# Windowed attention of the hybrid layers: from single steps of full-array products to pairs of steps of 64-row and 64-column tiles

## The reference

```python
# 8 query heads of 64, 2 key/value heads, blocks of 128 tokens
scores = jnp.einsum('bnqhgd,bnkhd->bnhgqk', qb, kcat).astype(jnp.float32)   # own block and the one before
scores = jnp.where(valid[None, :, None, None], scores * (HEAD_DIM ** -0.5), MASK_VALUE)
probs = jax.nn.softmax(jnp.concatenate([scores, sink], axis=-1), axis=-1)[..., :-1]
out = jnp.einsum('bnhgqk,bnkhd->bnqhgd', probs.astype(v.dtype), vcat)
...
gates = jax.nn.sigmoid(gate_logits)         # one of the projections of x, in three branches
merged = gates0 * (o_a @ w_a) + gates1 * (o_b @ w_b) + gates2 * (o_c @ w_c)
x = layer_norm(ALPHA * x + merged @ w_o)    # then the gated, convolved MLP
```

## Time and profile before

| | us |
|---|---|
| median of 3 runs | 2805.62 (2803.07 to 2809.05) |
| the profiled execution, its own time | 2806.11 |
| its span in the trace | 2804.3 |
| PE busy | 2785.4 |
| ACT busy | 1760.6 |
| DVE busy | 1698.9 |

### The profile page before, as it was taken

How to read it: one execution, slowest core, us unless ns; L and a number is a source line. 1 busy time by engine, 2 the same in 40 slices (tenths; PEclk the granted TensorE clock), 3 DMA queues, 4 the chain that set the end, 5 groups by cost and what they waited for, 6 DMA issues and landing times.

```text
span 2804.3 us, 42771 instructions
## 1 busy us (share of the span) xinstructions
PE 2785.4 (99%) x15770; PEld 2436.0 (87%) x15770; DVE 1698.9 (61%) x3003; ACT 1760.6 (63%) x2565; POOL 408.3 (15%) x472
## 2 busy tenths in 40 slices
PE   9999999999999999999999999999999999999999
PEld 7989889889998688899988898799988889789997
DVE  6654637354553773644547675678848766657864
ACT  7666767566655774565656755666656765566664
POOL 1111111111111001111111111111111011111110
PEclk9999999999999999999999999999999999999999
DMA  9766768688888327888886688788887578798885
GB/s 249 165 151 146 170 134 176 143 198 188 191 185 199 78 59 178 183 192 189 191 191 147 143 191 192 176 179 191 197 194 173 119 171 186 174 199 182 193 195 114
DMA packets 137038, 481.66 MB, mean 172 GB/s; under 512 B 15344, under 2 KB 15600, under 8 KB 136720
## 3 DMA queue, kind: packets, MB, share of 16 engines
q0 software_dynamic: 67296, 227.77, 46.3%
q1 hardware_dynamic: 68688, 249.59, 30.2%
q10 hardware_dynamic: 864, 1.72, 0.2%
HBM read 476.92 MB, written 2.10 MB: 171 GB/s over the span
## 4 chain that ended last, share of the span: by engine, by line
PE 98%; ACT 1%; DVE 1%; issue 0%; DVEq 0%; ACTq 0%
PE ps L1513 49%; PE ps L1689 24%; PE ps L1532 5%; PE ps L1965 3%; PE ps L2036 3%; PE ps L2091 2%; PE ps L1632 1%; PE ps L1902 1%; PE ps L2138 1%; PE ps L2116 1%; PE ps L1487 1%; PE ps L1809 1%; PE ps L1593 1%; PE ps L1615 0%; PE ps L1891 0%; PE ps L1590 0%
## 5 line engine op out<-in xcount | busy, mean ns | idle before, releaser
L573 ACT ACTIVATE wh<-raw 128x1024 fp32r<-128x1024 f32 (+2 forms) x461 | 455.5, 988 | 570.2 <-PE ps L1513 431.6
L556 POOL DMA_DIRECT2D wl<-weights x465 | 406.4, 874 | 2361.2 <-ACT wl L578 2301.4
L578 ACT ACTIVATE wl<-raw 128x1024 fp32r<-128x1024 f32 (+2 forms) x461 | 450.8, 978 | 0.0
L1513 PE MATMUL ps<-HH,wh 128*128 128x512 f32 x1088 | 427.2, 393 | 1.5 <-issue 1.3
L1513 PE MATMUL ps<-HH,wl 128*128 128x512 f32 x1088 | 423.8, 390 | 0.0
L1513 PE MATMUL ps<-HL,wh 128*128 128x512 f32 x1088 | 423.6, 389 | 0.0
L1513 PE MATMUL ps<-MH,wh 128*128 128x512 f32 x928 | 362.4, 390 | 2.9 <-issue 2.2
L1513 PE MATMUL ps<-MH,wl 128*128 128x512 f32 x928 | 361.2, 389 | 0.0
L1513 PE MATMUL ps<-ML,wh 128*128 128x512 f32 x928 | 361.1, 389 | 0.0
L1513 PEld LDWEIGHTS ps<-HH,wh 128*128 128x128 f32 x1088 | 204.3, 188 | 45.9 <-issue 4.0
L1513 PEld LDWEIGHTS ps<-HH,wl 128*128 128x128 f32 x1088 | 204.2, 188 | 43.0
(11 more groups left out here) (452 smaller groups left out, 5673.7 us busy)
## 6 DMA issues: line engine op xcount, KB each, us to landing
raw<-weights SPq DMA_DIRECT2D x468, 512.0 KB, 5.1
wl<-weights POOLq DMA_DIRECT2D x329, 512.0 KB, 7.9
wl<-weights POOLq DMA_DIRECT2D x136, 384.0 KB, 6.6
XT<-x SPq DMA_DIRECT2D x4, 512.0 KB, 8.3
arena<-tables POOLq DMA_DIRECT2D x1, 1024.0 KB, 11.0
out<-XT SPq DMA_DIRECT2D x1, 768.0 KB, 3.3
out<-XT SPq DMA_DIRECT2D x3, 256.0 KB, 2.4
arena<-table_h ACTq DMA_DIRECT2D x1, 640.0 KB, 5.9
```

The costliest lines, as they stand in the source:

```text
L556: pool.dma_start(wl[:, n, first:], weights[slab][:, first:], accum_op=ALU.add).then_inc(w_lo[n], 16)
L573: act_f(wh[:, n, at:w], raw[:, n, at:w], ACT.Copy)
L578: act_f(wl[:, n, at:w], raw[:, n, at:w], ACT.Identity, scale=-1.0).then_inc(w_hi, 1)
L1513: op = mm(bank(g, t), w[:, slot, at:at + P], x[:, first + kt, :], start=(kt == 0 and w is wh and x is xh), stop=(kt == n_k - 1 and w is wl ...
```

## The change

The 16 steps become 8 pairs of steps (two token blocks of one query tile).

- Scores: the key tile is one tile kH with both heads' rows and no zeros. Each head's product contracts its own 64 rows, so the two heads' products stand in different halves of the array's rows. Head h writes PSUM bank 4 + h, step s of the pair at column 256 s.
- Outputs: each head's product writes 64 columns of the array (64 partitions of PSUM) and takes only that head's 64 value columns. The two steps of a pair lie beside each other in one bank.
- Semaphores, statistics and copies go by pairs: the statistics are 4 columns wide where they were 2, the copies out of PSUM, the rounding and the low part 256 columns where they were 128. The exponentials and the transposes stay by step.
- The probability buffers are four where they were three. The scores' two banks are the same for each pair, where before they alternated.
- On PE a pair issues: its scores, the outputs of the pair two before, a gate tile, the transpose of a step of the pair before, a gate tile, the other transpose. Four memsets on DVE (the zeros) are gone.

```diff
-    return 2 if i < 4 else 1 if i <= H_STEPS else 0
+    return (4, 0, 0) if pair == 0 else (3, 0, 0) if pair == 1 else (1, 1, 0) if pair < H_PAIRS else (1, 1, 1)
...
-            return ps[:, h_bank(g, 4 + j % 2), h * w:(h + 1) * w]
+            return ps[:, h_bank(g, 4 + h), 256 * s:256 * s + w]
...
+                    else:
+                        pe.wait_ge(att_m, (a + 2 * pair).value(0))
+                    for s, n in h_steps(pair):
+                        keys = slice(max(n - 1, 0) * P, (n + 1) * P)
+                        for h in range(2):
+                            rows = slice(64 * h, 64 * h + 64)
+                            op = mm(h_scores(gate, s, h, h_width(n)), qh[rows, t, n * P:(n + 1) * P], kH[rows, keys],
+                                    start=True, stop=True)
+                    op.then_inc(att_s, 2)
...
+                def outputs(pair):
+                    pe.wait_ge(att_c, (a + 2 * pair).value(2))
+                    if pair > 0:
+                        pe.wait_ge(att_out, hl.times(H_STEPS).value(2 * pair))
+                    for s, n in h_steps(pair):
+                        per = h_width(n) // P
+                        for k in range(per):
+                            for h in range(2):
+                                at, cols = (h * per + k) * P, slice(64 * h, 64 * h + 64)
+                                op = mm(h_out(gate)[cols, s * P:(s + 1) * P], vzH[:, h, n - per + 1 + k, cols],
+                                        pTH[:, s, at:at + P], start=(k == 0), stop=(k == per - 1))
+                    op.then_inc(att_o, 2)
...
-                for i in range(H_STEPS + 3):
-                    if i < H_STEPS:
-                        score(i)
-                    done = gate_tiles(done, gate_tiles_at(i))
-                    if 2 <= i < H_STEPS + 2:
-                        transpose(i - 2)
-                    if i >= 3:
-                        output(i - 3)
-                    if i == H_STEPS + 1:
-                        gate_tiles(done, 1)
+                for pair in range(H_PAIRS + 2):
+                    tiles_at = gate_tiles_at(pair) if pair <= H_PAIRS else (0, 0, 0)
+                    if pair < H_PAIRS:
+                        scores(pair)
+                    if pair >= 2:
+                        outputs(pair - 2)
+                    done = gate_tiles(done, tiles_at[0])
+                    if 1 <= pair <= H_PAIRS:
+                        transpose(2 * pair - 2)
+                    done = gate_tiles(done, tiles_at[1])
+                    if 1 <= pair <= H_PAIRS:
+                        transpose(2 * pair - 1)
+                    done = gate_tiles(done, tiles_at[2])
...
+                for pair in range(H_PAIRS + 2):
+                    if pair < H_PAIRS:
+                        most(pair)
+                    if pair <= H_PAIRS:
+                        stats(pair if pair < H_PAIRS else None, pair - 1 if pair else None)
+                    for work in beside.get(pair, ()):
+                        work()
+                    if pair >= 2:
+                        low_parts(pair - 2)
```

More of the change, by code:

```diff
@@ L96 @@
 H_STEPS = 16
+H_PAIRS = H_STEPS // 2
+H_STATS = ("most", "less", "sum", "sink", "gap")
 HALVES = (slice(0, 256), slice(256, 512))
@@ L439, in h_out @@
             base = h_bank(g, 7) * S
-            return psf[:, base:base + P]
+            return psf[:, base:base + 2 * P]
         def a_window(i):
@@ L2104, in mix, with scores @@
                             .then_inc(mix_done, 1)
[L2106 to L2110 removed]
+                def scores(pair):
+                    t = pair // 2
+                    if pair == 0:
                         pe.wait_ge(qh_done, hl.times(5).value(5))
                         pe.wait_ge(mix_taken, hl.times(2).value(2))
[L2113 to L2121 removed]
+                    else:
[7 more added lines that the diff above has]
+                    op.then_inc(att_s, 2)
                 def transpose(j):
@@ new lines, in _, with most @@
+                a = c.take("att", H_STEPS)
+                def most(pair):
+                    dve.wait_ge(att_s, (a + 2 * pair).value(2))
+                    held(dve, dve_held)
+                    for k, n in h_steps(pair):
+                        w = h_width(n)
+                        for h in range(2):
+                            v.tensor_tensor_reduce(out=smH[(2 * pair + k) % 4][:, h * w:(h + 1) * w],
+                                                   in0=h_scores(gate, k, h, w), in1=mask_h[:, 256 - w:256], scale=1.0,
+                                                   scalar=NEG, op0=ALU.add, op1=ALU.max,
+                                                   accum_out=h_stat(pair, "most")[:, 2 * k + h:2 * k + h + 1])
@@ new lines, in stats @@
+                def stats(here, before):
+                    if here is not None:
+                        at = L_SINK + 2 * (here // 2)
+                        sink = lpar[:, at:at + 2].unsqueeze(1).broadcast_to((P, 2, 2))
+                        mx, gap = (h_stat(here, kind).rearrange("p (s h) -> p s h", h=2) for kind in ("most", "gap"))
+                    if before is not None:
+                        den = h_stat(before, "sum")
+                        dve.wait_ge(att_e, (a + 2 * before).value(2))
+                        v.tensor_tensor(den, den, h_stat(before, "sink"), ALU.add)
@@ L3225, in _ @@
-                for i in range(H_STEPS + 4):
-                    if i < H_STEPS:
-                        dve.wait_ge(att_s, (a + i).value(1))
-                        held(dve, dve_held)
-                    if i <= H_STEPS:
-                        softmax(i, i < H_STEPS and (lambda h, w: h_scores(gate, i, h, w)),
-                                i > 0 and (lambda: dve.wait_ge(att_e, (a + i).value(0))))
-                    if i in beside:
-                        beside[i]()
-                    if i >= 4:
-                        low_part(i - 4)
+                    if here is not None:
+                        v.tensor_tensor(gap, sink, mx, ALU.subtract)
+                        v.tensor_scalar(h_stat(here, "less"), h_stat(here, "most"), -1.0, None, ALU.mult).then_inc(att_m, 2)
```

167 lines of the change are left out of this document (64 added, 103 removed).

## The result

The changed kernel takes **2818.92 us** (median of 6 runs, 2817.83 to 2820.35), the one before 2805.57 beside it (6 runs, 2803.07 to 2809.05). The ratio is 1.0047, with a 95% interval of 1.0034 to 1.0060: slower, by 13.4 us. I had forecast 5.8 more, 2811.5 in all, with a range up to 2825. The side is right and the number lies in the range, but the step is more than twice the one that I had summed.

What follows compares the result with a forecast made beforehand. PE bounds attention now; afterwards a loop through DVE and ACT would: 4.6, 33.8 and 10.9 give 49.3 us a layer, with 0.7 for mode changes 50.0 against 47.1. Over two layers 5.8 more: 2811.5 us, range 2802 to 2825.

Steps and rivals of the forecast that it cites:

- the change of mode: Entering tiled products on PE may drain the array: 0 to 0.17 us each, 0.7 a layer taken as the middle.
- The loop: Scores, maxima, statistics, normalisation, transposes, next scores through PE, DVE and ACT: 11.25 us for four steps against 10.47 before.
- its waits for the normalisation: In each pair PE waits 1 to 1.4 us for DVE's normalisation ahead of the first transpose.
- the end of the layer: After the last pair's scores, the remaining copies, exponentials, transposes and outputs of a layer's attention: 10.9 us.
- The wait for ACT's copy ahead of the second transposes: In each pair PE waits 0.2 to 0.3 us for ACT's copy of the first step's transposes.
- Only the neighbours of different heads overlap: On PE a head's second record waits for its first, so scores need 5 of 8 slots, outputs 9 of 16.
- the first rival: Both heads' tiles overlap fully and the drain is free: 47.5 us a layer, 2807 in all; chance 0.22.
- what costs nothing: Work said to add no time: removed memsets and key split on DVE, ACT's merged copies and slab table, weight DMA.
- tiles that don't overlap: Rival: the two heads' products on PE run one after another, 8.9 us more a layer, 2823; chance 0.20.
- a clock that falls three times a layer: Rival: PE's share of work in attention is too low for full clock, 4.5 us a layer, 2821; chance 0.06.
- Faster, once the waits overlap more than their rows say: Rival: ACT and PE work bound the layer at some 40 us, 7 less: 2791; chance 0.12.

Runs made afterwards that it cites:

- Experiment 1: The changed kernel with DVE's low part of the gated tiles behind the third pair's statistics instead of the second's: 2812.71 us.
- experiment 3: The kernel before with only its outputs as 64-column tiles, no pairs, scores of the whole array: 2802.27 us against 2805.78 of before.
- experiment 4: The changed kernel with all of the first head's tiled products before the second's, per pair for scores, per step for outputs: 2819.50 us.
- scores ahead: The changed kernel with six probability buffers and the next pair's scores issued on PE ahead of the transposes: 2816.04 us.
- before, col 40: The kernel before with its small tile of statistics 40 columns wide instead of 32, the 8 more unused: 2809.02 us against 2804.71.
- ahead, full outputs: The 2797.56 us kernel (scores and a gate tile ahead of what waits, statistics' tile behind the arena) with outputs as full-array products again: 2808.13 us.
- col 64: The changed kernel with the tile of statistics 64 columns wide instead of 40: 2823.62 us.
- statistics behind: The changed kernel with its statistics in a tile of their own behind the arena, which lies where it lay before the change: 2814.90 us.

## Why the prediction was right in its sign and short in its size

**The attention without mishaps.** The forecast was 49.3 us and 0.7 for the change of mode, 50.0. Experiment 1, which has the loop and nothing else, takes 49.44. The loop (11.25), its waits for the normalisation (1.0 to 1.06), and the end of the layer stand. The wait for ACT's copy ahead of the second transposes, forecast at 0.2 to 0.3, shows as a distance of 0.39 instead of 0.23 behind the gate tile's last product, and as idle time nowhere: the tail of a record, 0.16 us, hides the start of each wait. PE's busy time in experiment 1's attention is 41.1 us and its idle time 8.3 (49.40 less 41.13), where I had some 37 and up to 13. By my estimate half of that is such tails, at some fifteen waits, and the rest work that I had too low, the changes of mode above all.

**PE's work: two terms wrong, and nearly equal, by luck.** "Only the neighbours of different heads overlap", 5/8 and 9/16, fell: the heads overlap in full, as the first rival had it. That makes the scores 0.25 and 0.17 us shorter than I had them. In the same group the change of mode costs more: the second transposes take 0.59 up to the scores instead of 0.43, and the first slot of scores 0.32 instead of 0.21. Together 0.27, and the last slot has 0.10 more; I had taken 0.09 of a bound of 0.17. So the groups of scores ended near where I had put them, 1.06 and 0.87 against 1.09 and 0.82, for another reason. What the transposes take more is paid back by links that are a little shorter than I had them: DVE starts the maxima 0.27 behind the scores and not 0.35 (timeline of DVE; the next record on PE starts at 1548.07):

```profile
1548.34 0.43 DVE L3203 CUSTOM_DVE_ANT_0 arena<-ps,arena 128x256 f32<-128x256 f32 x1 [2.52 <-PE ps L2131]
```

The sum came out right with wrong terms, and the changed kernel's loop alone would not have shown it. The Trainium skill (TensorEngine Tiling (Array Packing), Key Properties) says that a change of mode drains the engine; the traces fit it, with 0.17 for each change in experiment 3 and 0.27 ahead of the scores here. The Trainium skill (TensorE: Matmul & The Clock Gate, Measured speedup vs the span model) also counts some 4 ns for each further tile; the trace agrees nearly, with the two heads' records starting 6 to 7 ns apart, both records of an fp32 product alike.

**The step that failed: under "what costs nothing" I had only the table on ACT ("keeps its place in the loop").** The table on DVE is missing there. The table of slab work on ACT nearly kept its place, but beside it ACT's high part of the gated tiles went from step 2 to the end of pair 1. On DVE gated_lows went from the fourth of sixteen steps to the second of eight pairs, ahead of the maxima of pair 2, while ACT writes the high part that it waits for only at the end of its own pair 1, behind its exponentials and two copies. 2 x 1.45 us of wait and 2 x 1.37 of clock are 5.6 us in the profiled execution; by the medians experiment 1 gives 6.2.

**A term that was not there: the arena's place.** 32 bytes cost 4.1 to 4.3 us by the traces (1.3 to 1.5 ahead of the first attention with stop and clock taken out, 1.3 between, 1.5 behind), 4.3 and 3.3 by the medians of the two kernels that differ from their like in it alone, the second not clear of the noise. It is part of the change (col from 32 to 40 columns), and the prediction has no term for it. No row of before could have priced it.

**The sum.** The span grew by 12.8 us: two attentions, 10.3, of which 5.6 are the low part and the clock and 4.7 the loop (I had 5.8 for it, with the change of mode); 1.5, 1.9 and 1.5 outside them; less the 2.4 us by which the one stop of PE was longer in before's execution. The medians, 13.4 apart, are near it. That 2818.9 lies in the range at all is luck: its upper end was set by tiles that don't overlap and by a clock that falls three times a layer, and neither came; the low part and the arena's place filled that room.

**The clock.** I gave its fall 0.06, for PE's thin work in each pair. That is not what it fell behind: in the steady loop it never fell; one fall a layer came behind the wait of 2.5 us, and not each time.

**The rivals.** "The tiles don't overlap" fell by experiment 4's rows. "Faster, once the waits overlap more than their rows say" fell for this order (11.25 against the 10.1 from which it decides), and came true for another: with scores and a gate tile ahead of what waits, the loop is 9.3, and the kernel 2797.6.

## What to carry to other kernels

Work that is merged into wider steps moves everything that stood between the steps: list what each engine's table now places where, and for each entry who writes what it waits for and when, before costing the loop. A saving on the engine that bounds is worth its price only in an order that keeps feeding it: put independent work between each product and the copy of it that the next product needs, and issue the next round's first product ahead of what waits. And when a kernel changes in time in code that nobody touched, look at what moved in memory; keeping the small tile that grew behind the large one took the drift away here.

## What the runs showed that I had not expected

- The start of a large tile in SBUF, moved by 32 bytes, changes products with 256 moving columns in it from 278 to 286 ns, by 128 bytes to 290, and the kernel by 4 and some 9 us. No sign of it inside the attention.
- PE stops for up to 2.3 us between two products of the same line (1142.51) in some traces and not in others, in code that is the same. The waits view names nobody, but the landing of a weight transfer ends it, 9.2 to 9.6 us after its issue where the stop is 1.7 us or more and 6.7 to 8.1 elsewhere. In three of the six traces with such a long stop (scores ahead; before, col 40; ahead, full outputs) the clock fell behind it as well, at 1.6 us more with col 40. A difference of 2 us between two traces needs a look for such a stop first.
- The same wait of 2.5 us with the same order of work around it was followed by the lower clock in six attentions of eight (52.3 to 52.5 us long) and not in two (50.9): the changed kernel, head by head, col 64, and the statistics behind.
- Two tiled fp32 products in different row halves start 0.006 us apart with the heads taken in turn and 0.014 head by head, with the same slots, and a change between tiled and full products costs 0.17 to 0.27 us, where eight output records of two heads save 0.45.
